# Modulation vectors made inside three other phases, in blocks of 128 columns

## The chip, the cores and the metric

The kernel runs on one core of a Trainium2 chip. The metric is the device time of one execution in microseconds (us): the kernel before took 4822.7 us, the median of three runs (4816.3 to 4823.88). Engines are named as in the profile: PE multiplies matrices (PEld is its weight load), DVE, ACT and POOL work on vectors, and SP starts most transfers (its queue is SPq).

## The reference, cut to what matters

The program is three transformer blocks on 1024 tokens of width 1024. The second block is modulated by a conditioning vector:

```
sc, scc = silu(c), silu(c_ctx)                  # two vectors of 1024
mx = sc @ w_mod + b_mod                         # w_mod is 1024 x 6144
mc = scc @ w_mod + b_mod
sh1, sc1, g1, sh2, sc2, g2 = split(mx, 6)
csh1, csc1 = first two pieces of mc
hc = modulate(rms_norm(ctx, norm1_g), csh1, csc1)      # keys and values of 256 context tokens
hx = modulate(rms_norm(x, norm1_g), sh1, sc1)
x = x + g1 * mixer(hx, ...)                     # attention, long convolution, Fourier mixing
h2 = modulate(rms_norm(x, norm2_g), sh2, sc2)
x = x + g2 * experts(h2)
```

The first block has a gated short convolution, `b * conv3(c * u)` over 256 channels. In the mixer of the second block the heads of queries and keys are each normalised over 64 channels, multiplied by a gain and rotated (`u * cos + rotated(u) * sin`). Its long convolution starts with filters made by a small network with two sine layers, times a decay, and divided by the sum of their absolute values.

## The kernel before, in words

The program is a row of phases. Each phase writes one instruction list for every engine; the lists meet at the phase's end, and the next phase starts after it. Nothing of one phase runs beside the next, so what a phase costs is set by the last of its engines. Semaphores order the work within a phase.

Four stages matter here. The first is `short_conv_phase` (name `conv`, L1603), near the end of the first block: SP loads coefficients and six tiles of 128x1024, DVE does ten operations on them, ACT stores two results. PE has no work in it.

The second is `mod_phase` (`mod`, L1730), ahead of the second block's context. It makes all 6144 columns of both vectors. The weights come in twelve tiles of 128x8x512 (2048 KB each, L1755). For each tile PE holds 128x2 numbers of silu(c) as weights and streams the 128x512 tile past them, eight times (L1779). DVE adds the bias to the 2x512 result (L1798), PE turns it with four small products (L1785), and DVE copies the turned columns into `cols` (L1801), which later phases read as 48 blocks of 128.

The third is three phases in a row: `load_phase` (`b2_tables`, L1590: cosines, sines and two copies of the values), `norm_phase` (`qk_norm`, L290: for each of ten half rows ACT squares, PE sums with a 128x128 matrix of ones blocks at L390, DVE, ACT, ACT and DVE finish), and `rope_phase` (`qk_rope`, L1688: PE moves the pairs at L1706, DVE multiplies and adds, SP stores).

The fourth is `hyena_filter_phase` (`filter`, L1837). PE makes two layers of 64x1024 (L1940); DVE reduces the angles and ACT takes the sine after each (L2047). ACT and POOL split eight raw tables meanwhile (L2032, L2070): ACT's list holds four of those splits ahead of each sine. Then PE goes through eight chunks: filter taps of chunk i (L1955, 64-row weights) and sums of absolute values of chunk i-1 (L1946); DVE multiplies by the decay (L2000) and ACT takes the absolute value (L2063). SP's list starts the tables, the decays and a 4096 KB copy of `xT` to memory (`x_spill`) in a fixed order.

All products in these stages take 32-bit floats. Each such instruction shows as two records on PE and two weight loads in the trace.

Of the kernel before, what the change touches and what calls it, by code (L numbers as in the profile page):

```python
# [11 lines left out]
ALU = mybir.AluOpType  # L12
ACT = mybir.ActivationFunctionType
AX = mybir.AxisListType
P = 128
T = 1024
# [1586 lines left out]
def short_conv_phase(nc, name, n_pairs, src, gate_before, gate_after, w, b, left, out):  # L1603

    n_chunks = 2 * n_pairs
    with Phase(nc, name) as ph:
        taps, bias = ph.sb("taps", [P, n_chunks, 3]), ph.sb("bias", [P, n_chunks])
        z = [ph.sb(f"z{s}", [P, T + 2]) for s in range(2)]  # L1610
        before = [ph.sb(f"before{s}", [P, T]) for s in range(2)]
        after = [ph.sb(f"after{s}", [P, T]) for s in range(2)]
        acc = [ph.sb(f"acc{s}", [P, T]) for s in range(2)]
        coef_loaded, padded = ph.sem("coef_loaded"), ph.sem("padded")
        loaded, used = [ph.sem(f"loaded{s}") for s in range(2)], [ph.sem(f"used{s}") for s in range(2)]
        stored, done = [ph.sem(f"stored{s}") for s in range(2)], ph.sem("done")
        block = ph.block()
        n_in = 1 + (gate_before is not None) + (gate_after is not None)
        n_ops = 3 + (gate_before is not None) + (gate_after is not None)

        @block.sync
        def _(sp):
            for i in range(3):
                sp.dma_start(taps[:, :, i], w[i].rearrange("(c p) -> p c", p=P),
                             allow_slow_non_contiguous=True).then_inc(coef_loaded, 16)
            load_columns(sp, bias[:, :], b, coef_loaded)

            def load(i, s):
                sp.dma_start(z[s][:, left:left + T], src(i * 2 + s)).then_inc(loaded[s], 16)
                if gate_before is not None:  # L1630
                    sp.dma_start(before[s][:, :], gate_before(i * 2 + s)).then_inc(loaded[s], 16)
                if gate_after is not None:
                    sp.dma_start(after[s][:, :], gate_after(i * 2 + s)).then_inc(loaded[s], 16)

            for s in range(2):
                load(0, s)
            if n_pairs > 1:
                with sp.Fori(1, n_pairs) as i:
                    for s in range(2):
                        sp.wait_ge(used[s], i)  # L1640
                        load(i, s)

        @block.vector
        def _(dve):
            for s in range(2):
                if left:
                    nc.vector.memset(z[s][:, 0:left], 0.0).then_inc(padded, 1)
                if left < 2:
                    nc.vector.memset(z[s][:, left + T:], 0.0).then_inc(padded, 1)
            dve.wait_ge(padded, 2 * ((left > 0) + (left < 2)))  # L1650
            dve.wait_ge(coef_loaded, 16 * 4)
            for s in range(2):
                dve.sem_inc(stored[s], 16)
            with dve.Fori(0, n_pairs) as i:
                for s in range(2):
                    op = 0

                    def link(ins):
                        nonlocal op
                        op += 1  # L1660
                        ins.then_inc(done, 1)
                        dve.wait_ge(done, i * (2 * n_ops) + (s * n_ops + op))

                    dve.wait_ge(loaded[s], i * (16 * n_in) + 16 * n_in)
                    if gate_before is not None:
                        link(nc.vector.tensor_tensor(z[s][:, left:left + T], z[s][:, left:left + T], before[s][:, :], ALU.mult))
                    dve.wait_ge(stored[s], i * 16 + 16)
                    tap = lambda n: taps[:, ds(i * 2 + s, 1), n]
                    link(nc.vector.tensor_scalar(acc[s][:, :], z[s][:, 0:T], tap(0), bias[:, ds(i * 2 + s, 1)],
                                                 ALU.mult, ALU.add))  # L1670
                    for n in (1, 2):
                        link(nc.vector.scalar_tensor_tensor(out=acc[s][:, :], in0=z[s][:, n:n + T], scalar=tap(n),
                                                            in1=acc[s][:, :], op0=ALU.mult, op1=ALU.add))
                    if gate_after is not None:
                        link(nc.vector.tensor_tensor(acc[s][:, :], acc[s][:, :], after[s][:, :], ALU.mult))
                    dve.sem_inc(used[s], 1)

        @block.scalar
        def _(act):
            with act.Fori(0, n_pairs) as i:  # L1680
                for s in range(2):
                    act.wait_ge(used[s], i + 1)
                    act.dma_start(out(i * 2 + s), acc[s][:, :].rearrange("p (o t) -> p o t", o=1)).then_inc(stored[s], 16)
            for s in range(2):
                act.wait_ge(stored[s], 16 * n_pairs + 16)
# [44 lines left out]
def mod_phase(nc, name, ident, c_rows, w_mod, b_mod, cols):  # L1730

    N = w_mod.shape[1]
    n_pairs = N // HALF // 2
    w_view = w_mod.rearrange("(c p) n -> p c n", p=P)
    with Phase(nc, name) as ph:
        cond, sig, silu = ph.sb("cond", [P, KD, 2]), ph.sb("sig", [P, KD, 2]), ph.sb("silu", [P, KD, 2])
        w_sb = [ph.sb(f"w{s}", [P, KD, HALF]) for s in range(2)]
        bias = [ph.sb(f"bias{s}", [2, HALF]) for s in range(2)]
        rows = [ph.sb(f"rows{s}", [2, HALF]) for s in range(2)]
        acc = [ph.ps(f"acc{s}", [2, HALF]) for s in range(2)]  # L1740
        turned = [ph.ps(f"turned{s}", [P, 4, 2]) for s in range(2)]
        cond_loaded, sig_ready, silu_ready = ph.sem("cond_loaded"), ph.sem("sig_ready"), ph.sem("silu_ready")
        loaded, acc_ready = [ph.sem(f"loaded{s}") for s in range(2)], [ph.sem(f"acc_ready{s}") for s in range(2)]
        rows_ready, turned_ready = [ph.sem(f"rows_ready{s}") for s in range(2)], [ph.sem(f"turned_ready{s}") for s in range(2)]
        cols_ready = [ph.sem(f"cols_ready{s}") for s in range(2)]
        block = ph.block()

        @block.sync
        def _(sp):
            for r in range(2):  # L1750
                sp.dma_start(cond[:, :, r], c_rows[r].rearrange("(c p) -> p c", p=P),
                             allow_slow_non_contiguous=True).then_inc(cond_loaded, 16)

            def load(i, s):
                sp.dma_start(w_sb[s][:, :, :], w_view[:, :, ds((i * 2 + s) * HALF, HALF)]).then_inc(loaded[s], 16)  # L1755
                for r in range(2):
                    sp.dma_start(bias[s][r:r + 1, :], b_mod[0:1, ds((i * 2 + s) * HALF, HALF)]).then_inc(loaded[s], 16)

            for s in range(2):
                load(0, s)  # L1760
            with sp.Fori(1, n_pairs) as i:
                for s in range(2):
                    sp.wait_ge(rows_ready[s], i)
                    load(i, s)

        @block.scalar
        def _(act):
            act.wait_ge(cond_loaded, 32)
            nc.scalar.activation(sig[:, :, :], cond[:, :, :], ACT.Sigmoid).then_inc(sig_ready, 1)

        @block.tensor
        def _(pe):
            pe.wait_ge(silu_ready, 1)
            with pe.Fori(0, n_pairs) as i:
                for s in range(2):
                    pe.wait_ge(loaded[s], i * 48 + 48)
                    pe.wait_ge(cols_ready[s], i + 1)
                    for c in range(KD):
                        mm = nc.tensor.matmul(acc[s][:, :], silu[:, c, :], w_sb[s][:, c, :], start=(c == 0), stop=(c == KD - 1))  # L1779
                    mm.then_inc(acc_ready[s], 1)  # L1780
                for s in range(2):
                    pe.wait_ge(silu_ready, 1)
                    pe.wait_ge(rows_ready[s], i + 1)
                    for b in range(4):
                        tr = nc.tensor.matmul(turned[s][:, b, :], rows[s][:, b * P:(b + 1) * P], ident[0:2, 0:2],  # L1785
                                              start=True, stop=True)
                    tr.then_inc(turned_ready[s], 1)
# [3020 lines left out]
```

## Time and profile before

| | us |
|---|---|
| median of three runs | 4822.7 |
| the profiled execution | 4812.0 |
| its span, first to last instruction | 4810.1 |
| PE busy | 3956.5 (82%) |
| DVE busy | 2735.6 (57%) |
| ACT busy | 1976.4 (41%) |

The profile is of one execution, whose own time (4812.0) is 1.9 us over its span and 10.7 us under the median. Since phases don't overlap, a stage is read by its own start and end, and by what its engines wait for between them. The granted clock of PE is a number between 0 and 1: 0.50 is 1.2 GHz, 1.00 is 2.4 GHz, and numbers between are stretches with both. The page's own chain of what ended last breaks off after a few per cent, so the stages below are read from the time lines.

### The profile page before, as it was taken

To read this page: it belongs to the slowest core of one execution; us is meant where nothing else is said; L and a number is where in the kernel's file an instruction comes from. 1 tells how busy PE (TensorE), PEld (TensorE's weight loads), DVE (VectorE), ACT (ScalarE), POOL (GpSimd) and SP (SyncE) were. 2 spreads that over 40 slices of the span, in tenths; PEclk is the share of its full clock that TensorE was granted. 3 is DMA by queue.
4 is the path that set the end of the run, shared out by engine and by line. 5 is a ranking of instruction groups with operands and counts; after the bars stand their busy time and mean duration, and the time that the engine had idled before them with its cause. 6 is when DMAs were issued, how large, how long until landed. Compare 5 with 4: busy or idle time off the path is not lost. (4 is left out here: it accounts for less than half of the span.)

```text
span 4810.1 us, 51648 instructions
## 1 busy us (share of the span) xinstructions
PE 3956.5 (82%) x18534; PEld 3124.2 (65%) x18534; DVE 2735.6 (57%) x3196; ACT 1976.4 (41%) x2670; POOL 470.4 (10%) x349
## 2 busy tenths in 40 slices
PE   7995756959997797698948999999996997474489
PEld 5884535427885576386746888888885785353477
DVE  4124756132112676675566999999996322445952
ACT  2113543031112465324315777777774112354323
POOL 1000012015000121200000011000100400000010
PEclk8997878979998899799958999999997998787789
DMA  3223122422222201416318999999995222424241
GB/s 94 96 87 89 49 86 60 158 92 79 96 96 80 58 24 37 163 72 206 101 71 341 401 383 380 382 393 381 382 381 187 78 93 95 157 76 120 54 143 67
DMA packets 437325, 768.37 MB, mean 160 GB/s; under 512 B 104895, under 2 KB 260799, under 8 KB 436024
## 3 DMA queue, kind: packets, MB, share of 16 engines
q1 hardware_dynamic: 406760, 686.74, 40.8%
q10 hardware_dynamic: 25808, 62.92, 3.4%
q0 software_dynamic: 4608, 16.78, 1.3%
q8 instruction: 87, 1.43, 0.1%
q14 instruction: 62, 0.51, 0.0%
HBM read 644.85 MB, written 115.87 MB: 158 GB/s over the span
## 5 line engine op out<-in xcount | busy, mean ns | idle before, releaser
L71 PE MATMUL b_in_acc<-b_in_acts_hi,b_in_w_hi 128*128 128x512 f32 (+1 forms) x1456 | 580.4, 399 | 48.4 <-POOL b_in_acts_lo L749 20.6
L72 PE MATMUL b_in_acc<-b_in_acts_lo,b_in_w_hi 128*128 128x512 f32 (+1 forms) x1456 | 573.7, 394 | 0.0
L73 PE MATMUL b_in_acc<-b_in_acts_hi,b_in_w_lo 128*128 128x512 f32 (+1 forms) x1456 | 573.4, 394 | 0.0
L3354 DVE TENSOR_TENSOR experts_w_lo<-top_xT,experts_w_hi 128x2048 fp32r<-128x2048 f32 x192 | 437.4, 2290 | 62.7 <-ACT experts_w_hi L3299 62.7
L66 DVE CAST b_in_w_hi<-b_in_w 128x1024 fp32r<-128x1024 f32 (+1 forms) x91 | 68.0, 750 | 702.0 <-PE b_in_acc L73 702.0
L3354 DVE TENSOR_TENSOR experts_w_lo<-experts_ring,experts_w_hi 128x2048 fp32r<-128x2048 f32 x192 | 435.8, 2288 | 31.8 <-ACT experts_w_hi L3299 29.6
L559 ACT ACTIVATE b_in_out<-b_in_acc 128x512 f32<-128x512 f32 (+1 forms) x182 | 108.9, 599 | 810.8 <-PE b_in_acc L73 808.7
L3299 ACT ACTIVATE experts_w_hi<-top_xT 128x2048 fp32r<-128x2048 f32 x192 | 367.5, 1919 | 126.9 <-PE experts_gate L73 74.8
L3299 ACT ACTIVATE experts_w_hi<-experts_ring 128x2048 fp32r<-128x2048 f32 x192 | 367.7, 1921 | 115.0 <-PE experts_up L73 65.0
L71 PEld LDWEIGHTS b_in_acc<-b_in_acts_hi,b_in_w_hi 128*128 128x128 f32 (+1 forms) x1456 | 275.6, 189 | 129.3 <-POOL b_in_acts_lo L749 34.8
L73 PEld LDWEIGHTS b_in_acc<-b_in_acts_hi,b_in_w_lo 128*128 128x128 f32 (+1 forms) x1456 | 276.6, 190 | 59.1
L72 PEld LDWEIGHTS b_in_acc<-b_in_acts_lo,b_in_w_hi 128*128 128x128 f32 (+1 forms) x1456 | 276.8, 190 | 56.8 <-issue 0.7
L71 PE MATMUL experts_gate<-experts_w_hi,experts_xg_hi 128*128 128x512 f32 x512 | 202.1, 395 | 4.8 <-DVE experts_w_lo L3354 4.8
L71 PE MATMUL experts_y_ps<-experts_w_hi,experts_act_hi 128*128 128x512 f32 x512 | 205.5, 401 | 0.0
L71 PE MATMUL experts_up<-experts_w_hi,experts_xg_hi 128*128 128x512 f32 x512 | 200.9, 392 | 2.7 <-DVE experts_w_lo L3354 2.7
L73 PE MATMUL experts_gate<-experts_w_hi,experts_xg_lo 128*128 128x512 f32 x512 | 200.5, 392 | 0.0
L73 PE MATMUL experts_y_ps<-experts_w_hi,experts_act_lo 128*128 128x512 f32 x512 | 200.4, 391 | 0.0
L72 PE MATMUL experts_gate<-experts_w_lo,experts_xg_hi 128*128 128x512 f32 x512 | 200.4, 391 | 0.0
L72 PE MATMUL experts_y_ps<-experts_w_lo,experts_act_hi 128*128 128x512 f32 x512 | 199.8, 390 | 0.0
L73 PE MATMUL experts_up<-experts_w_hi,experts_xg_lo 128*128 128x512 f32 x512 | 199.5, 390 | 0.0
L72 PE MATMUL experts_up<-experts_w_lo,experts_xg_hi 128*128 128x512 f32 x512 | 199.5, 390 | 0.0
L1235 ACT ACTIVATE gqa_pT_hi<-gqa_turned 128x512 fp32r<-128x512 f32 (+1 forms) x192 | 94.4, 531 | 86.4 <-PE gqa_turned L1159 86.2
(677 smaller groups left out, 8656.4 us busy)
## 6 DMA issues: line engine op xcount, KB each, us to landing
experts_ring<-in_w_gate SPq DMA_DIRECT2D x128, 1024.0 KB, 7.4
top_xT<-in_w_up SPq DMA_DIRECT2D x128, 1024.0 KB, 9.9
experts_ring<-in_w_down SPq DMA_DIRECT2D x64, 1024.0 KB, 9.6
top_xT<-in_w_down SPq DMA_DIRECT2D x64, 1024.0 KB, 9.3
b_in_w<-in_w_in SPq DMA_DIRECT2D x90, 512.0 KB, 3.9
proj<-b_in_out ACTq DMA_DIRECT2D x90, 512.0 KB, 2.7
mod_w<-in_w_mod SPq DMA_DIRECT2D x12, 2048.0 KB
x_spill<-top_xT SPq DMA_DIRECT2D x3, 4096.0 KB, 14.0
```

The source lines that it names most:

```text
L66: return nc.vector.tensor_copy(hi, x)
L71: nc.tensor.matmul(out, w_hi, x_hi, start=start, stop=False)
L72: nc.tensor.matmul(out, w_hi, x_lo, start=False, stop=False)
L73: return nc.tensor.matmul(out, w_lo, x_hi, start=False, stop=stop)
L559: nc.scalar.activation(out, acc[s][h][0:m, :], ACT.Sigmoid if gated else ACT.Copy).then_inc(ready, 1)
L1235: nc.scalar.activation(pT_hi[m % 2][:, b0:b0 + bn, t0:t0 + P], turned[x % 2][:, 0:bn, :], ACT.Copy).then_inc(hi_ready, 1)
L3299: nc.scalar.activation(w_hi[n % HIS][:, :, :], ring[n % RING], ACT.Copy).then_inc(hi_ready, 1)
L3354: nc.vector.tensor_tensor(w_lo[n % HIS][:, :, :], ring[n % RING], w_hi[n % HIS][:, :, :].bitcast(F32), ALU.subtract).then_inc(lo_ready, 1)
```

## The change

`mod_phase` is gone. `cols`, `silu` and `bias` are now held for the whole run of the first two blocks, and the twelve tiles are made by three other phases, four each. A helper does a block of 128 columns the other way round: the 128x128 block of `w_mod` is PE's weights, and the 128x2 numbers of silu are streamed past. The result lies in columns at once, without a turn.

```
+MOD_STEPS = (4, 4, 4)
+def modulation_block(nc, acc, w, silu, b):
+    for c in range(KD):
+        mm = nc.tensor.matmul(acc, w[:, c, b * P:(b + 1) * P], silu[:, :, c], start=(c == 0), stop=(c == KD - 1))
+    return mm
```

The short convolution's phase becomes `conv_modulation_phase`. It turns the bias and both conditioning vectors with one product, makes silu, and PE does tiles 0 to 3. DVE writes the convolution's result straight into `y`.

```
+        @block.tensor
+        def _(pe):
+            pe.wait_ge(vec_loaded, 48)
+            nc.tensor.transpose(turned[:, :], vec_rows[:, :], ident[0:NB + 2 * KD, 0:NB + 2 * KD]).then_inc(vec_turned, 1)
+            pe.wait_ge(silu_ready, 1)
+            for n in range(n_steps):
+                pe.wait_ge(w_loaded[n % RING], 16 * (n // RING + 1))
+                for b in range(4):
+                    mm = modulation_block(nc, made[n][:, b, :], w[n % RING], silu, b)
+                mm.then_inc(made_ready, 1)
```

SP's list in this phase, before; all of it but the coefficients is the convolution's inputs:

```order
L1624 DMA conv_taps<-in_conv_w 128x2x1 x3
L767 DMA conv_bias<-in_conv_b 128x2x1
L1629 DMA conv_z<-proj 128x1024
L1631 DMA conv_before<-proj 128x1024
L1633 DMA conv_after<-proj 128x1024
```

And now; `conv_w` is a tile of `w_mod`, `conv_vec_rows` holds the bias and the two vectors:

```order
L1643 DMA conv_vec_rows<-in_b_mod 48x128
L1645 DMA conv_vec_rows<-in_c 8x128
L1645 DMA conv_vec_rows<-in_c_ctx 8x128
L1637 DMA conv_w<-in_w_mod 128x8x512
L1641 DMA conv_z<-proj 128x1024
L1641 DMA conv_before<-proj 128x1024
L1641 DMA conv_after<-proj 128x1024
L1649 DMA conv_taps<-in_conv_w 128x2x1 x3
```

The first weight tile now stands ahead of the convolution's inputs, and the fourth waits until PE has done the first.

`query_key_phase` (`qk`) does the work of `b2_tables`, `qk_norm` and `qk_rope` in one phase, half row by half row, with 16 blocks (tiles 4 to 7) spread between its products:

```
+            for j in range(NU):
+                pe.wait_ge(square_ready, j + 1)
+                if j >= 2:
+                    pe.wait_ge(log_ready, j - 1)
+                nc.tensor.matmul(sums[j % 2][:, :], block_ones[:, :], square[j % 2][:, :], start=True, stop=True).then_inc(sums_ready, 1)
+                modulation(part(j, 0))
+                if j >= 1:
+                    rotate(j - 1)
+                modulation(part(j, 1))
+            rotate(NU - 1)
```

PE's list here, before and now, the first rows; `qk_sums` is the sum of squares, `qk_moved` the rotation, `qk_made` a modulation block:

```order
-L381 UNCONDITIONAL_BRANCH
-L390 MATMUL qk_norm_sums<-qk_norm_square,top_squares 128x512 x10
-L39 UNCONDITIONAL_BRANCH
-L1701 UNCONDITIONAL_BRANCH
-L1706 MATMUL qk_rope_moved<-b2q_qk,top_squares 128x512 x10
+L1790 UNCONDITIONAL_BRANCH
+L1812 MATMUL qk_sums<-qk_square,top_squares 128x512
+L1609 MATMUL qk_made<-modulation_silu,qk_w 128x2 x8
+L1812 MATMUL qk_sums<-qk_square,top_squares 128x512
+L1609 MATMUL qk_made<-modulation_silu,qk_w 128x2 x8
+L1806 MATMUL qk_moved<-qk_xn,top_squares 128x512
+L1609 MATMUL qk_made<-modulation_silu,qk_w 128x2 x8
```

The two runs of ten products become a mixture with eight small products after nearly every large one. ACT now takes the logarithm of the sums directly (scale 1/64, added eps), and DVE's ten mean operations are gone.

`hyena_filter_phase` gets tiles 8 to 11 as eight half tiles of 1024 KB. The loads stand in SP's list, and PE calls `modulation(n)` after each of the two layers and in chunks 1 to 6:

```
             for c in range(2):
                 load_line(c)
+            for n in range(2):
+                load_mod(n)
             for j in range(4):
                 load_raw(j)
+            load_mod(2)
             for i in range(2):
                 load_decay(i)
...
                 if i >= 1:
                     sizes(i - 1)
+                if i in (1, 2, 3, 4, 5, 6):
+                    modulation(i + 1)
...
+            dve.wait_ge(mod_used, 2 * n_steps)
+            nc.vector.tensor_tensor(cols[...], made[:, :, :], mod_bias[...], ALU.add).then_inc(cols_made, 1)
```

PE's list in the filter phase, before, from the first layer; `filter_pre` is a layer, `filter_norm` the sum of absolute values:

```order
L1940 MATMUL filter_pre<-filter_feats,filter_w 64x512 x2
L1940 MATMUL filter_pre<-filter_hidden,filter_w 64x512 x2
L1955 MATMUL filter_taps<-filter_w,filter_hidden 128x512 x4
L1946 MATMUL filter_norm<-filter_size,top_squares 128x512 x2
L1955 MATMUL filter_taps<-filter_w,filter_hidden 128x512 x2
```

And the same stretch now:

```order
L2060 MATMUL filter_pre<-filter_feats,filter_w 64x512 x2
L1609 MATMUL filter_made<-modulation_silu,filter_mod_w 128x2 x16
L2060 MATMUL filter_pre<-filter_hidden,filter_w 64x512 x2
L1609 MATMUL filter_made<-modulation_silu,filter_mod_w 128x2 x16
L2076 MATMUL filter_taps<-filter_w,filter_hidden 128x512 x4
L2067 MATMUL filter_norm<-filter_size,top_squares 128x512 x2
L1609 MATMUL filter_made<-modulation_silu,filter_mod_w 128x2 x16
L2076 MATMUL filter_taps<-filter_w,filter_hidden 128x512 x2
```

Sixteen small products now stand between the sums of one chunk and the taps of the next, six times.

## Rows read from the trace of the kernel before

**Rows 1.** The page, its head and part 1: busy us, share, instructions.

```profile
span 4810.1 us, 51648 instructions
PE 3956.5 (82%) x18534; PEld 3124.2 (65%) x18534; DVE 2735.6 (57%) x3196; ACT 1976.4 (41%) x2670; POOL 470.4 (10%) x349
```

**Rows 2.** Windows: the four stages, from their first instruction to the next stage's.

```profile
core 0: us, PE busy (x) PEld busy (x) DVE busy (x) ACT busy (x) POOL busy (x), PEclk, DMA share, GB/s
663.29:687.35 24.06, 0.00 (x0) 0.00 (x0) 11.76 (x12) 0.00 (x0) 0.00 (x0) 0.50 0.48 175
886.59:994.28 107.69, 96.30 (x288) 26.80 (x288) 10.32 (x25) 1.50 (x2) 0.00 (x0) 0.95 0.68 234
1516.64:1583.00 66.36, 30.10 (x40) 8.67 (x40) 32.74 (x50) 18.97 (x31) 0.00 (x0) 0.66 0.28 105
1908.84:1996.76 87.92, 45.03 (x74) 14.64 (x74) 72.20 (x63) 27.30 (x25) 23.89 (x8) 0.67 0.56 199
```

**Rows 3.** Time line of mod: start us, us, engine, line, operation, records [idle before].

```profile
887.64 0.57 SPq L1755 DMA_DIRECT2D mod_w<-in_w_mod  x1
896.23 15.23 PE L1779 MATMUL mod_acc<-mod_w,mod_silu 128*2 128x512 f32 x32 [10.64 <-DMA mod_bias<-in_b_mod]
991.73 1.95 PE L1785 MATMUL mod_turned<-top_squares,mod_rows 2*128 2x2 f32 x16
```

**Rows 4.** Time line and windows of the two long runs of small products.

```profile
2426.04 27.49 PE L3069 MATMUL route_logits<-route_w,b2r_hT 128*128 128x16 f32 x128 [16.20 <-DMA route_w<-in_w_router]
2514.23 27.44 PE L3091 MATMUL route_picked<-route_facts,route_sel 128*128 128x4 f32 x128 [4.64 <-DVE route_sel L3149]
2426.04:2453.53 27.49, 27.49 (x128) 27.38 (x128) 0.00 (x0) 0.00 (x0) 0.00 (x0) 0.50 0.27 116
2514.23:2541.67 27.44, 27.44 (x128) 27.36 (x128) 15.27 (x7) 0.00 (x0) 0.00 (x0) 0.50 0.00 1
```

**Rows 5.** Time line of PE in the last phase: eight small records, twice.

```profile
4688.22 0.95 PE L4297 MATMUL last_col<-top_squares,last_square 128*128 128x1 f32 x8
4694.81 1.87 PE L4297 MATMUL last_col<-top_squares,last_square 128*128 128x1 f32 x8 [2.75 <-ACT last_square L4382]
```

**Rows 6.** Time line of conv: DVE's first product, the next phase's first load.

```profile
663.29 1.41 SPq L1624 DMA_DIRECT2D conv_taps<-in_conv_w  x3
671.79 1.23 DVE L1666 TENSOR_TENSOR conv_z<-conv_z,conv_before 128x1024 f32<-128x1024 f32 x1 [8.32 <-DMA conv_after<-proj]
687.35 1.14 SPq L1088 DMA_DIRECT2D mem_k_raw<-mem_kv  x2
```

**Rows 7.** Time line and window of the norm and rotation.

```profile
1548.81 1.10 PE L390 MATMUL qk_norm_sums<-qk_norm_square,top_squares 128*128 128x512 f32 x2 [1.10 <-ACT qk_norm_square L352]
1579.32 0.69 DVE L1719 TENSOR_TENSOR qk_rope_out<-qk_rope_cos_part,qk_rope_sin_part 128x512 f32<-128x512 f32 x1
1563.00:1577.00 14.00, 9.26 (x16) 2.37 (x15) 13.76 (x23) 0.00 (x0) 0.00 (x0) 0.94 0.27 112
```

**Rows 8.** Time line of the filter phase.

```profile
1922.08 1.06 ACT L2032 ACTIVATE hy_table_hi<-filter_raw 128x1024 fp32r<-128x1024 f32 x1 [1.47 <-DMA filter_raw<-in_half_tables]
1926.20 1.06 ACT L2032 ACTIVATE hy_table_hi<-filter_raw 128x1024 fp32r<-128x1024 f32 x1 [0.26 <-DMA filter_raw<-in_half_tables]
1929.79 1.06 ACT L2047 ACTIVATE filter_hidden<-filter_hidden 64x1024 f32<-64x1024 f32 x1 [1.23 <-DVE filter_hidden L1833]
1948.64 1.06 ACT L2047 ACTIVATE filter_hidden<-filter_hidden 64x1024 f32<-64x1024 f32 x1 [2.28 <-DVE filter_hidden L1833]
1949.75 7.19 PE L1955 MATMUL filter_taps<-filter_w,filter_hidden 64*128 64x512 f32 x8 [15.18 <-ACT filter_hidden L2047]
1960.91 1.99 PE L1955 MATMUL filter_taps<-filter_w,filter_hidden 64*128 64x512 f32 x4
1987.30 3.31 PE L1946 MATMUL filter_norm<-filter_size,top_squares 128*128 128x512 f32 x4 [2.78 <-ACT filter_size L2063]
1990.72 0.69 DVE L2015 TENSOR_SCALAR filter_total<-filter_norm 128x512 f32<-128x512 f32 x1 [3.24 <-PE filter_norm L1946]
```

More of the change, by code:

```diff
@@ L1608, in short_conv_phase @@
     with Phase(nc, name) as ph:
-        taps, bias = ph.sb("taps", [P, n_chunks, 3]), ph.sb("bias", [P, n_chunks])
+        taps, taps_bias = ph.sb("taps", [P, 2, 3]), ph.sb("taps_bias", [P, 2])
         z = [ph.sb(f"z{s}", [P, T + 2]) for s in range(2)]
[L1611 to L1614, printed above, removed]
@@ L1615, in short_conv_phase @@
-        loaded, used = [ph.sem(f"loaded{s}") for s in range(2)], [ph.sem(f"used{s}") for s in range(2)]
-        stored, done = [ph.sem(f"stored{s}") for s in range(2)], ph.sem("done")
+        before, after, acc = ([ph.sb(f"{n}{s}", [P, T]) for s in range(2)] for n in ("before", "after", "acc"))
+        vec_rows, sig = ph.sb("vec_rows", [NB + 2 * KD, P]), ph.sb("sig", [P, 2 * KD])
+        w = [ph.sb(f"w{s}", [P, KD, HALF]) for s in range(RING)]
+        turned = ph.ps("turned", [P, NB + 2 * KD])
@@ L1635, in _ @@
[L1635 to L1641, printed above, removed]
+            load_columns(sp, taps_bias[:, :], taps_b, coef_loaded)
+            load_w(1)
+            load_chunk(1)
+            for n in range(2, n_steps):
+                load_w(n)
+        @block.tensor
[8 more added lines that the diff above has]
+                mm.then_inc(made_ready, 1)
@@ L1651, in _ @@
-            dve.wait_ge(coef_loaded, 16 * 4)
-            for s in range(2):
[L1653 to L1676, printed above, removed]
@@ L1678, in _, with squares @@
         @block.scalar
         def _(act):
[L1680 to L1685, printed above, removed]
+            act.preload_act_table_set("natural_log_exp_and_others")
+            def squares(j):
+                act.wait_ge(x_loaded[j // 2], 16)
+                if j >= 2:
+                    act.wait_ge(sums_ready, j - 1)
+                nc.scalar.activation(square[j % 2][:, :], x[j // 2][:, at(j)], ACT.Square).then_inc(square_ready, 1)
@@ L1727, in _ @@
             sp.wait_ge(stored, 16 * len(chunks))
[L1730 to L1787, printed above, removed]
-        @block.vector
-        def _(dve):
-            dve.wait_ge(sig_ready, 1)
-            nc.vector.tensor_tensor(silu[:, :, :], sig[:, :, :], cond[:, :, :], ALU.mult).then_inc(silu_ready, 1)
-            for s in range(2):
-                dve.sem_inc(cols_ready[s], 1)
-            with dve.Fori(0, n_pairs) as i:
-                for s in range(2):
-                    dve.wait_ge(acc_ready[s], i + 1)
-                    nc.vector.tensor_tensor(rows[s][:, :], acc[s][:, :], bias[s][:, :], ALU.add).then_inc(rows_ready[s], 1)
-                for s in range(2):
-                    dve.wait_ge(turned_ready[s], i + 1)
-                    nc.vector.tensor_copy(cols[:, ds((i * 2 + s) * 4, 4), :], turned[s][:, :, :]).then_inc(cols_ready[s], 1)
@@ L1908, in _ @@
                 load_line(c)
+            for n in range(2):
+                load_mod(n)
             for j in range(4):
                 load_raw(j)
+            load_mod(2)
             for i in range(2):
@@ L1934, in _, with modulation @@
         def _(pe):
+            def modulation(n):
+                pe.wait_ge(mod_loaded[n % 3], 16 * (n // 3 + 1))
+                for b in range(2):
+                    mm = modulation_block(nc, made[:, 2 * n + b, :], mod_w[n % 3], silu, b)
+                mm.then_inc(mod_used, 1)
             pe.wait_ge(loaded, 16 * 7)
```

247 lines of the change are left out of this document (208 added, 39 removed).

## The prediction

> **What bounds the kernel now.** I read the page's head first: PE is busy 82% of the span [rows 1]. That is a mean over stages; what counts here are four stages which the change touches, so I took windows over them [rows 2]. The reader is to see that PE does nothing in conv (24.1 us), is busy in nearly all of mod (96.3 of 107.7 us), and is busy in about half of the other two (30.1 of 66.4 and 45.0 of 87.9). The phases don't overlap, so 107.7 us can go, if the work fits into PE's free time elsewhere: 24.1 + 36.3 + 42.9, together 103 us. The question is how long this work takes in its new form, and for that I looked for the nearest products in the time line: 128x128 weights with a few columns streamed [rows 4, 5]. Last I read the time lines of the receiving stages for what their ends wait for [rows 6 to 8].
>
> **What a block costs.** In mod one record with 512 columns comes each 0.43 us (16 of a tile in 7; the first 32 took 15.23 with a slow start) [rows 3]. The new form has 8 products for a block of 128 columns, 16 records, 64 for a tile, 768 for all. The nearest run is `route_logits`: 128x128 float weights, 16 columns streamed, sums over eight pieces; 128 records in 27.49 us, 0.215 us each. `route_picked`, with 4 columns, takes 27.44 [rows 4]. Both ran at a granted clock of 0.50 (1.2 GHz) from first to last, with no idle time in them. At 1.00 (2.4 GHz) the same kind costs half: eight `last_col` records take 0.95 us, 0.12 each, against 1.87 after 2.75 us of idleness [rows 5], and 16 turns with 2 columns in mod take 1.95, after 0.25 for the last to come out about 0.114 each [rows 3]. So a tile costs 64 x 0.215 = 13.8 us at the low level and 64 x 0.114 = 7.3 at the high one; all twelve cost 165 or 88 us. The low price alone is over the 107.7 that goes.
>
> Which level? PE idles before conv, before the queries' phase and before the filters, all three begin at the low level [rows 2, 6, 8], and both route runs stayed there for 27 us though PE never paused [rows 4]. I take the low level for runs of small products.
>
> The Trainium skill ("TensorE: Matmul & The Clock Gate", "Why this matters for your kernels") advises to keep TensorE continuously busy to get the full clock. Read so, conv's 256 records would lift it; route's rows speak against this, since weight loads and matmuls there were back to back at 0.50. The same page's section "LDWEIGHTS (loading the stationary operand)" gives a load's time by its columns alone, about 107 ns for 128; by two such loads for a float product even the high clock would leave 0.21 us a record. Rows 5 differ with 0.12, and the measurement decides.
>
> **Part by part.** *mod removed*: -107.7 us, from its first load to the next phase's [rows 2]. What follows it waits for its own load and starts at the low level either way.
>
> *conv*: now three small loads stand first, so the first tile's load is issued at 663.3 + 3 x 0.47 = 664.7. In mod the tile's load was issued at 887.64 and PE began at 896.23, 8.6 us later [rows 3]; so PE begins here at 673.3. The turn and silu are done by then (their three loads are small). The second tile has 13.8 us to come, behind 1.5 MB of inputs; 2 MB take about 5.5 us at the rate of the filter's raw tables (three steps of 0.5 MB from 1922.08 to 1926.20, 1.37 each [rows 8]), so PE doesn't wait again. Four tiles: 55.0, to 728.3; DVE's last addition and the change of phase 0.7, to 729.0. The stage takes 65.7, **+41.6 us**. The convolution's DVE work (11.8 us [rows 2]) lies beside it, and costs nothing. At the high level it would be 29.2 for the tiles, +16.
>
> *queries and keys*: loads of x, gains (0.6 each) and the first tile are issued by 1519.5; with mod's 8.6 the first block starts at about 1527.5 to 1528. Behind it PE has 16 blocks x 3.44 = 55.0 and 19 large products (sums 1 to 9 and ten rotations) of two records. A record with 512 columns takes 0.857 at the low level (7.19 us for eight, less 0.33 for the last to come out [rows 8]) and 0.43 at the high (1.99 for four); so 19 x 1.71 = 32.5. PE is the bound: DVE needs 4 operations of about 0.7 for a half row, ACT three of 0.6, against 8.8 on PE. PE ends at 1615.0, two DVE operations later (1.7) the last store is issued, and it needs the same 3.0 us to the next phase as before (1579.32 + 0.69 to 1583.00 [rows 2, 7]). Next phase at 1619.7, +36.7. The rounds which I merge (two phase changes, ten mean operations, gains that came last) are in this, since I build the stage anew. A large product now seldom has another beside it, only three times are two together. In the norm the level was high for short stretches after such runs (1.10 us for two records [rows 7]), so I take off 4: **+33 us**. With all at the high level: 16 x 1.83 + 19 x 0.86 = 45.6 behind 1527.5, the end at 1577.8, -5.
>
> Rotation's window shows that PE can keep the high level with pauses, once it has it (9.3 of 14 us busy, 0.94 [rows 7]); a small product streams 2 columns where those streamed 512, so I don't count on it.
>
> *filters*: first the loads. Two half tiles (2 MB, 5.5 us) go ahead of the raw tables and a third ahead of the decays and the 4 MB copy. ACT's fourth table split moves from 1926.20 to 1931.7, with the table load and its own time the first sine starts at 1934.1 instead of 1929.79; the second, behind the last four tables, 8 us later: 1956 instead of 1948.64. It costs 7.5 because ACT's list keeps the splits ahead of the sine; DVE's angles, which were the last to come, are early now. modulation(0) and (1) lie in PE's waits for the sines and cost nothing. Then the loop: first taps at 1957.3; 8 x 4 + 8 x 4 records of 0.857 are 54.9, six half tiles of 6.9 are 41.3; PE ends at 2053.5, and after the same 6.1 us (1990.6 to 1996.76) the phase at 2059.6: +62.9 with all at the low level. Before, the loop was at the high level from 1960.9 on (1.99 us for four), and low again at 1987.30 after 2.78 us of idleness [rows 8]. Now 6.9 us of large records stand together in each round. I estimate that in two rounds of three the level rises at their end and is lost within the 6.9 us of small ones, with about 3.4 saved each time: 14 off, **+49 us**. High throughout: 7.1 us a round, +25.
>
> Sum: -107.7 + 41.6 + 33 + 49 = **+16 us**. The profiled execution would go from 4812.0 to 4828, and the median, 10.7 above it, to 4839.
>
> **Rivals.** *The small products run high beside large ones.* In conv PE stays low, in the other two stages the large products lift the clock and it holds: -107.7 + 41.6 - 5 + 25 = -46, 4777. For it: rotation's window and the loop's high level. Against it: the level was gone after 2.78 us without a product [rows 8]. The sign of the whole turns where a tile's mean cost falls by 16/12 = 1.3 us, to 12.5.
>
> *Every run of small products is lifted*, conv's too, as the rule cited would have it: -107.7 + 16 - 5 + 25 = -72, 4751. Against it stand both route runs. It decides more than anything else here: 88 us for the small products or 165.
>
> *The loads bind.* The clock never rises in the three stages, and the filter's half tiles, with pieces of 1 KB instead of 2, come more slowly: +42 + 37 + 63 = 142, or +34 with the removal, and up to 10 more if the second sine moves by as much; 4857 to 4867.
>
> *No change*: the filter's loop is high in each round's large part (-22 instead of -14), queries 10 off: about +2 to +5, 4826.
>
> **How the numbers follow.** Low level with some rises 0.60 (its own range 4825 to 4858), loads and no rises 0.12, near no change 0.10, high beside large products 0.12, high everywhere 0.06. The likeliest gives 4839. The range goes from 4788 to 4866: it leaves out the last and most of the one before, and a little above. About 0.2% (9.6 us) is what a measurement can tell: faster 0.20, same 0.15, slower 0.65.
>
> **What would show it.** conv 65 us long, PE busy in 55 of it at a clock of 0.50, 256 small records with 0.215 from one to the next. The queries' phase 98 to 103 us, clock under 0.65, PE busy through. First and second sine 4 and 7 us later against the phase's start; rounds of 11 to 13.7 us in the loop; the filter phase 125 to 150. Wrong it is if the clock in conv is near 1.00, or if the merged phases end under 80 us.

## The result and the profile after

The changed kernel took 4826.0 us (median of 20 runs, 4815.7 to 4833.2) against 4819.1 for the kernel before (20 runs, 4809.7 to 4831.1). The ratio is 1.0016 with a 95% interval of 1.0009 to 1.0023: slower by some 7 us. That is less than the 0.2% (9.6 us) which the prediction had set as what can be told, though the interval lies wholly above 1. The forecast was +16. The profiled execution took 4825.94 us. Its page, head and part 1, to be held against [rows 1]:

```profile
span 4824.2 us, 52429 instructions
PE 4035.5 (84%) x19015; PEld 3257.8 (68%) x19015; DVE 2707.3 (56%) x3173; ACT 1974.8 (41%) x2669; POOL 463.5 (10%) x349
```

Windows over the three stages that are left, with the columns of [rows 2]: conv, queries and keys, filters.

```profile
665.79:730.48 64.69, 55.11 (x257) 54.87 (x257) 12.71 (x18) 0.18 (x1) 0.00 (x0) 0.50 0.50 180
1452.60:1549.40 96.80, 83.13 (x296) 62.49 (x296) 28.49 (x45) 19.86 (x31) 0.00 (x0) 0.54 0.43 159
1875.90:2014.50 138.60, 108.89 (x330) 67.58 (x330) 56.74 (x64) 27.11 (x25) 18.69 (x8) 0.56 0.52 187
```

The columns to read are the length, PE's busy time and the granted clock behind POOL's column. The four stages took 286.0 us before [rows 2]; these three take 300.1. The difference, 14.1, is the whole difference of the two spans (4824.2 - 4810.1). In all three the clock is at or near 0.50, the lower level (1.2 GHz).

PE's time line in conv. The first tile is there 9.2 us after the stage began, and 256 records follow without a pause, 0.214 us each, as route's did [rows 4]:

```profile
667.94 0.36 PE L1660 MATMUL conv_turned<-top_squares,conv_vec_rows 64*128 64x64 f32 x1 [6.97 <-DMA conv_vec_rows<-in_c_ctx]
675.04 54.75 PE L1609 MATMUL conv_made<-modulation_silu,conv_w 128*128 128x2 f32 x256 [6.74 <-DMA conv_w<-in_w_mod]
```

PE's time line in the queries' and keys' phase, around one of the two places where the level rose. A block (16 records) takes 3.41 us, a large product 2.06; after two large ones together the next two blocks take 2.17 and 2.39, and then the level is low again:

```profile
1463.77 3.57 PE L1609 MATMUL qk_made<-modulation_silu,qk_w 128*128 128x2 f32 x16 [5.07 <-DMA qk_w<-in_w_mod]
...
1479.29 3.41 PE L1609 MATMUL qk_made<-modulation_silu,qk_w 128*128 128x2 f32 x16
1482.56 2.06 PE L1806 MATMUL qk_moved<-qk_xn,top_squares 128*128 128x512 f32 x2
1484.41 1.91 PE L1812 MATMUL qk_sums<-qk_square,top_squares 128*128 128x512 f32 x2
1486.12 2.17 PE L1609 MATMUL qk_made<-modulation_silu,qk_w 128*128 128x2 f32 x16
1488.14 1.10 PE L1806 MATMUL qk_moved<-qk_xn,top_squares 128*128 128x512 f32 x2
1489.08 2.39 PE L1609 MATMUL qk_made<-modulation_silu,qk_w 128*128 128x2 f32 x16
1491.34 2.05 PE L1812 MATMUL qk_sums<-qk_square,top_squares 128*128 128x512 f32 x2
```

PE's time line in the filters, a round of the loop at the low level and one in which the small products run at the high one. The rounds are 14.04 and 11.0 us long, and the four records of the taps take 3.78 where before they took 1.99 [rows 8]:

```profile
1945.87 6.83 PE L1609 MATMUL filter_made<-modulation_silu,filter_mod_w 128*128 128x2 f32 x32
1952.62 3.78 PE L2076 MATMUL filter_taps<-filter_w,filter_hidden 64*128 64x512 f32 x4
1956.33 3.78 PE L2067 MATMUL filter_norm<-filter_size,top_squares 128*128 128x512 f32 x4
1959.91 6.83 PE L1609 MATMUL filter_made<-modulation_silu,filter_mod_w 128*128 128x2 f32 x32
...
1973.95 4.08 PE L1609 MATMUL filter_made<-modulation_silu,filter_mod_w 128*128 128x2 f32 x32
1977.96 3.50 PE L2076 MATMUL filter_taps<-filter_w,filter_hidden 64*128 64x512 f32 x4
1981.39 3.78 PE L2067 MATMUL filter_norm<-filter_size,top_squares 128*128 128x512 f32 x4
1984.96 3.71 PE L1609 MATMUL filter_made<-modulation_silu,filter_mod_w 128*128 128x2 f32 x32
```

### The profile page after: what moved, and what is told of

Same layout as the page of the kernel before. It is cut to its first block and busy times, and to the rows that moved or that the text cites. A ratio compares the mean times of both kernels' runs of the same rounds, so it can differ in the third digit from the quotient of the medians.

```text
span 4824.2 us, 52429 instructions
## 1 busy us (share of the span) xinstructions
PE 4035.5 (84%) x19015; PEld 3257.8 (68%) x19015; DVE 2707.3 (56%) x3173; ACT 1974.8 (41%) x2669; POOL 463.5 (10%) x349
## 6 DMA issues: line engine op xcount, KB each, us to landing
x_spill<-top_xT SPq DMA_DIRECT2D x3, 4096.0 KB, 13.7
```

## The stages of every kernel that was profiled

Each number is a stage's length in us in one profiled execution, from its first instruction to the next stage's first. The names of the kernels are explained with the experiments.

| kernel | conv | mod | queries, keys | filters | sum |
|---|---|---|---|---|---|
| before | 24.1 | 107.7 | 66.4 | 87.9 | 286.0 |
| before, second | 24.4 | 115.5 | 66.5 | 87.8 | 294.2 |
| before, third | 24.1 | 111.9 | 65.3 | 96.0 | 297.3 |
| after | 64.7 | - | 96.8 | 138.6 | 300.1 |
| after, second | 64.6 | - | 96.5 | 135.8 | 296.9 |
| after, third | 64.7 | - | 96.7 | 141.0 | 302.4 |
| merge alone | 24.1 | 107.6 | 42.9 | 87.6 | 262.2 |
| 128 columns in conv | 46.4 | - | 93.4 | 141.1 | 280.9 |
| 128 columns in all | 46.3 | - | 63.8 | 110.4 | 220.5 |
| 64 columns in all | 64.8 | - | 63.7 | 110.1 | 238.6 |
| 16 columns in all | 64.6 | - | 96.8 | 140.8 | 302.2 |
| 128, loads later | 44.8 | - | 63.6 | 108.2 | 216.6 |

## Experiments

**Both kernels again.** No edit. Each kernel was profiled and timed once more, and then profiled in a third execution. They tell how far one profile speaks for a kernel. What was expected of the kernel before:

> The kernel before once more, as it is. It tells how far the profiled execution of before (4812.0 us, its stages 24.1 conv, 107.7 mod, 66.4 norm and rotation, 87.9 filters) speaks for other executions. Theory A (the four stages repeat, what differs is spread over stages that the change leaves alone): time ratio 1.000, the four stages within 2 us of these numbers in sum, whatever the whole execution takes. Theory B (one of the four stages of before is usually longer, because the level of the clock comes at other moments, and the first profile had a lucky one): the four together 5 to 10 us longer than 286.0, which would explain why the timed change is about 7 us where the two profiles differ by 14.

and of its third execution:

> The kernel before once more, one look. mod_phase took 107.7 us in one of its executions, 115.5 in another (the level fell for short stretches in five of six pairs of tiles), and 107.6 in merge_only, where the same phase stands. If both are usual, this look has one of them or a number between; conv 24, norm and rotation 66.4, filters 88 again within 0.5. If 115.5 was a rare disturbance, 107.7.

Measured: the second had a ratio of 1.0004 (0.9995 to 1.0013), 4816.0 us; the profiled executions' spans were 4815.8 and 4821.0. The four stages were not 286.0 but 294.2 and 297.3. Windows over mod in the second and, in another fence, over mod and the filters in the third:

```profile
882.20:997.70 115.50, 104.41 (x288) 27.91 (x288) 10.32 (x25) 1.50 (x2) 0.00 (x0) 0.88 0.63 218
```

```profile
887.50:999.40 111.90, 101.18 (x288) 27.36 (x288) 10.32 (x25) 1.50 (x2) 0.00 (x0) 0.91 0.64 225
1913.20:2009.20 96.00, 53.37 (x74) 16.95 (x74) 72.44 (x63) 27.34 (x25) 23.29 (x8) 0.59 0.51 182
```

The same records, a clock of 0.88 and 0.91 where it was 0.95 [rows 2], and PE busy for 104.4 and 101.2 us instead of 96.3. The time line of the second shows it by pairs of tiles: 32 records that took 14.0 at the high level take 15.59 in four pairs.

```profile
910.89 15.59 PE L1779 MATMUL mod_acc<-mod_w,mod_silu 128*2 128x512 f32 x32 [0.35 <-DMA mod_bias<-in_b_mod]
926.41 1.95 PE L1785 MATMUL mod_turned<-top_squares,mod_rows 2*128 2x2 f32 x16
928.42 13.97 PE L1779 MATMUL mod_acc<-mod_w,mod_silu 128*2 128x512 f32 x32
```

In the third, the filters' loop reached the high level only at the taps of chunk 4, not of chunk 2 as in [rows 8]:

```profile
1976.84 3.78 PE L1946 MATMUL filter_norm<-filter_size,top_squares 128*128 128x512 f32 x4
1980.55 2.41 PE L1955 MATMUL filter_taps<-filter_w,filter_hidden 64*128 64x512 f32 x4
1982.89 1.98 PE L1946 MATMUL filter_norm<-filter_size,top_squares 128*128 128x512 f32 x4
```

So Theory B held in kind, with 8 and 11 us where it had 5 to 10: the first profile was of an execution in which the touched stages were short. The expectation for the third, which had the filters at 88 again, missed: they too vary. The rest of the program is not fixed either: outside the four stages these three executions took 4524.1, 4521.6 and 4523.7 us.

Of the changed kernel the second execution was expected to show:

> The changed kernel once more, as it is. Theory A: ratio to before 1.001 to 1.002, stages again 64.7 (conv), 96.8 (queries and keys) and 138.6 (filters), within 1 us each but for the level's flips: in the filters three rounds of six were 3.3 us shorter, and if these flips come by chance the filters' stage would move by 3.3 or 6.6 us between executions. Theory B (the changed stages repeat exactly): 300.1 in sum to within 1 us, and the three short rounds are the same three.

and the third:

> The changed kernel once more, one look: conv 64.7 within 0.2; queries and keys 93 to 97; filters 135.8, 138.6 or 141 by the number of rounds in the loop of which the small products run at the high level (four, three or two of six, 3.3 us each); sum of the three 293 to 302, against 286 or 294 for the four stages of before. So a change between 0 and +16 us from one pair of executions to another, around a mean of about 8, as timed.

Measured: ratio 1.0025 (1.0015 to 1.0035); stages 296.9 and 302.4. Conv repeats to 0.1 us, queries and keys to 0.3; the filters move by about 2.8 us with each round whose small products run high (four of six in the second). In the third they took 141.0 with three such rounds; there the last eight records of the sums took 6.48 us instead of 4.87. The queries' and keys' phase moves too: with the same instructions it took 93.4 in the kernel "128 columns in conv" below. The means of three executions are 292.5 before and 299.8 after, +7.3; pair by pair the stages give +14.1, +2.7 and +5.1. The timed changes are +6.9, in the second set +11.3 (4823.8 against 4812.6 for 25 executions of before, or +7.9 against the 4816.0 of the 11 others), and in the third, of single executions, +11.4 and +15.4 (4834.3 against 4822.9 and 4818.9). The second pair ran on one chip and the third on another, so what share of the spread is the chip's is not told apart.

**The merge alone.** The kernel before, with one of the change's parts: the three phases of the queries and keys in one, without modulation.

```
-            load_phase(nc, "b2_tables", ...)
-            norm_phase(nc, "qk_norm", ...)
-            rope_phase(nc, "qk_rope", ...)
+        query_key_phase(nc, "qk", block_ones, C["pair_rot"], rows_of(p, Q2, 5), ..., rows_of(q) + [kx[:, 0:T]], copies)
```

> The kernel before with one part of the change alone: tables, norm and rotation of the queries and keys are one phase as in the changed kernel, but with no modulation in it; mod_phase, conv and the filters stay as before. The prediction put a gain of the merge only into its total for that stage (33 longer with four tiles at 13.8 in it). Theory A (the merge saves two phase changes and DVE's ten mean operations, and the coefficients come beside the tables; then DVE bounds it with four operations of 0.7 to 0.8 for each of ten half rows): stage 50 to 55 us instead of 66.4, ratio to before 0.997. Rival (with PE's products interleaved with waits the level stays low, sums and rotations alternate on a chain through four engines): 60 to 66, ratio 0.999 to 1.000. It also gives a third look at mod_phase, which was 107.7 in one execution of before and 115.5 in the other: Theory B expects one of these two or a value between.

Measured: 4790.1 us, ratio 0.9956 (0.9942 to 0.9969); the stage took 42.9, less than Theory A gave. Its window, and DVE's groups by line (busy us, mean ns | idle before):

```profile
1515.80:1558.70 42.90, 23.45 (x40) 7.46 (x40) 27.41 (x41) 19.76 (x31) 0.00 (x0) 0.82 0.42 162
```

```profile
L1792 DVE SCALAR_TENSOR_TENSOR qk_xn<-qk_x,qk_gains,qk_inv 128x512 f32<-128x512 f32 x10 | 7.5, 751 | 10.9 <-DMA qk_sin<-in_grid_sin 7.8 <-ACT qk_inv L1753 1.9
L1781 DVE TENSOR_TENSOR qk_out<-qk_cos_part,qk_sin_part 128x512 f32<-128x512 f32 x10 | 6.9, 693 | 1.0
```

DVE waits 7.8 us for the sine table and then goes with hardly a gap, some 3.0 us for a half row. PE's time line in the middle of the stage: the large products are at the high level, with 1.0 us of waiting in each round.

```profile
1537.06 1.12 PE L1761 MATMUL qk_moved<-qk_xn,top_squares 128*128 128x512 f32 x2 [1.02 <-DVE qk_xn L1792]
1538.03 1.02 PE L1767 MATMUL qk_sums<-qk_square,top_squares 128*128 128x512 f32 x2
```

The estimate of 50 to 55 had left DVE's start where it was. What follows is a price for the modulation in this phase: 96.8 - 42.9 = 53.9 us for four tiles, 13.5 each, the low level's price for the small products (13.7). That is a net price, since it holds the large products' slowing too, and what the small ones fill of PE's waits. The stage's +30.4 in the result is +53.9 for the modulation and -23.5 for the merge. All three places together pay 40.6 + 53.9 + 50.7 = 145 us for what mod did in 108 to 116.

**More columns in conv.** The changed kernel, but each small product streams its two columns 64 times over. Same weights, same number of records; the surplus lands in PSUM beside the wanted columns, and later blocks write over it.

```
-def modulation_block(nc, acc, w, silu, b):
+REPEATS = (64, 1, 1)
+def modulation_block(nc, made, at, w, silu, b, repeats):
     for c in range(KD):
-        mm = nc.tensor.matmul(acc, w[:, c, b * P:(b + 1) * P], silu[:, :, c], start=(c == 0), stop=(c == KD - 1))
+        moving = silu[:, :, c:c + 1].rearrange("p r o -> p o r").to_broadcast([P, repeats, 2])
+        mm = nc.tensor.matmul(made[:, 2 * at:2 * at + 2 * repeats].rearrange("p (k r) -> p k r", r=2),
+                              w[:, c, b * P:(b + 1) * P], moving, start=(c == 0), stop=(c == KD - 1))
```

> As the changed kernel, but in conv each small product streams its two columns 64 times over (128 columns instead of 2, the same weights, the same 256 records; the surplus lands in PSUM beside the wanted columns and is overwritten or left). Theory A (what keeps PE at 1.2 GHz in runs of small products is that so little is streamed; the loads of weights alone don't lift the level): PE reaches the high level in conv, its 256 records take 30 to 36 us instead of 54.75, the phase 40 to 46 instead of 64.7, the whole 20 us less than the changed kernel (4803 to 4808, ratio to before 0.997). Theory B (float products with 128x128 weights stay low as in the router, or PE has been idle too long before this phase): conv 64.7 again, ratio 1.0016 as for the changed kernel. Theory C (streaming more costs by the column): a record of 128 columns at the low level needs 0.214 us by the quarter of the 0.857 us for 512, so as much as now, and no more than 2 us are lost.

Measured: 4803.6 us, ratio 0.9982 (0.9973 to 0.9991). Conv took 46.4 instead of 64.7. PE's time line there:

```profile
669.01 9.63 PE L1611 MATMUL conv_made<-modulation_silu,conv_w 128*128 128x128 f32 x64 [6.50 <-DMA conv_w<-in_w_mod]
680.13 7.41 PE L1611 MATMUL conv_made<-modulation_silu,conv_w 128*128 128x128 f32 x64 [1.49 <-DMA conv_w<-in_w_mod]
689.39 16.19 PE L1611 MATMUL conv_made<-modulation_silu,conv_w 128*128 128x128 f32 x128 [1.85 <-DMA conv_w<-in_w_mod]
```

The second tile takes 7.41 us instead of 13.7: the small record is at 0.116 and the level is high. Sixty-four times the streamed data, and the time is halved. PE now waits 1.5 and 1.9 us for weights, the new second limit. Theories B and C are out.

**More columns everywhere.** The one line that differs is `REPEATS = (64, 64, 64)`.

> As wide_conv, with 128 columns streamed in all three phases. Theory A: conv -20, the queries' and keys' phase from 96.8 to about 66 (16 blocks at 1.83 instead of 3.41 and the large products at 0.86 instead of 1.71), the filters from 138.6 to 110 to 115; the whole 65 to 75 us under the changed kernel, 4750 to 4760, ratio to before 0.986 to 0.988, faster than before. Theory B: the same as the changed kernel within 3 us. A mixture (high only in conv, where nothing interrupts the run; in the other two the waits between the products break it): 4795 to 4805.

Measured: 4740.7 us (4737.6 to 4743.3), ratio 0.9849 (0.9835 to 0.9862), so 1.5% faster than before and 83 us under the changed kernel, more than the 65 to 75 of Theory A (its own parts add up to 75 to 80). The windows:

```profile
660.40:706.70 46.30, 33.56 (x257) 32.83 (x257) 12.62 (x18) 0.18 (x1) 0.00 (x0) 0.82 0.69 251
1428.50:1492.30 63.80, 50.22 (x296) 38.66 (x296) 27.89 (x45) 19.86 (x31) 0.00 (x0) 0.85 0.63 241
1817.90:1928.30 110.40, 78.18 (x330) 49.46 (x330) 56.71 (x64) 27.21 (x25) 18.68 (x8) 0.78 0.66 235
```

In the queries' phase blocks of 1.95 us stand between large products of 1.02 to the end; in the filters' loop it is 3.74 for a half tile between sums and taps of 1.99, rounds of 7.41 us. PE's time line, two rows of the one and then a round of the other:

```profile
1456.66 1.95 PE L1611 MATMUL qk_made<-modulation_silu,qk_w 128*128 128x128 f32 x16
1458.45 1.02 PE L1815 MATMUL qk_sums<-qk_square,top_squares 128*128 128x512 f32 x2
...
1889.68 3.74 PE L1611 MATMUL filter_made<-modulation_silu,filter_mod_w 128*128 128x128 f32 x32
1893.35 1.99 PE L2079 MATMUL filter_taps<-filter_w,filter_hidden 64*128 64x512 f32 x4
1895.27 1.98 PE L2070 MATMUL filter_norm<-filter_size,top_squares 128*128 128x512 f32 x4
```

The same instruction counts as in the result's windows, at clocks of 0.78 to 0.85 instead of 0.50 to 0.56.

**Sixteen and sixty-four columns.** `REPEATS = (8, 8, 8)` and `(32, 32, 32)`.

> As wide_all, but 16 columns streamed. Theory A (the level goes by what is streamed): nearly as the changed kernel with its 2, since the router's run with 16 columns stayed at 0.50: conv 64 to 65, ratio to before 1.001 to 1.002. The rival to it (it is not the amount, but that the moving operand is repeated or that the result is contiguous over many columns which made wide_all fast): as wide_all, 0.985.

> As wide_all, but 64 columns streamed instead of 128. If the high level needs streamed columns in proportion, the level is reached in part and the whole lies between 4741 and 4824; if 64 are enough it is 4741 within 5 us, with a small record at 0.114 as before, since its weight load then is what sets its time. The loss would be seen first in conv, where no large product helps.

Measured with 16: 4824.0 us, ratio 1.0017 (1.0008 to 1.0027), as the changed kernel; so the repeated operand and the longer rows in PSUM are not the cause; the kernels with 16 and with 128 columns differ in the number of columns streamed, and the room for them in PSUM, alone. With 64: 4759.7 us, ratio 0.9893 (0.9879 to 0.9908), neither the 4741 that 64 columns would give if they were enough everywhere nor the changed kernel's time. Of the stages the difference to 128 is conv alone, which stayed low from end to end while the two stages with large products between were as with 128. Windows over conv, first with 16 and then with 64 columns:

```profile
659.40:724.00 64.60, 55.13 (x257) 54.87 (x257) 12.71 (x18) 0.18 (x1) 0.00 (x0) 0.50 0.49 180
```

```profile
660.00:724.80 64.80, 55.21 (x257) 54.86 (x257) 12.70 (x18) 0.18 (x1) 0.00 (x0) 0.50 0.49 179
```

PEld is busy 54.9 of these 64.6 us, with weight loads back to back, and the level did not rise.

**The filters' loads elsewhere.** As with 128 columns in all, and in SP's list:

```
-            for n in range(2):
-                load_mod(n)
             for j in range(4):
                 load_raw(j)
-            load_mod(2)
+            for n in range(2):
+                load_mod(n)
...
             for j in range(4, NJ):
                 load_raw(j)
+            load_mod(2)
```

> As wide_all, with the modulation's loads in the filters' phase put elsewhere in SP's list: the first two half tiles behind the first four raw tables instead of ahead of them, the third behind the last four raw tables instead of ahead of the 4 MB copy. It tests the step on the sines (4 and 7 us later than in before by prediction, 4.0 and 4.3 measured). Theory A (the first sine is late by the 2 MB ahead of the raw tables, the second only by all the bytes ahead of the last tables): first sine 4 us earlier against the phase's start than in wide_all (21 instead of 25.2), the second 2.5 earlier (1 MB less ahead of it; 42 instead of 44.4), the phase 2 to 3 shorter, 108 instead of 110.4. Rival (the second sine waits for the first and for DVE's angles): both 4 earlier, the phase 106. Time 4738, no difference to wide_all that can be told from the whole.

Measured: 4737.3 us, ratio 0.9845 (0.9831 to 0.9859), not to be told from the version before it in the whole. Against the phase's start (1818.3) the sines stand at 20.8 and 42.2, as Theory A had it, and the phase takes 108.2. ACT's time line:

```profile
1836.62 1.28 ACT L2178 ACT_TABLE_LOAD   x1
1839.08 1.06 ACT L2178 ACTIVATE filter_hidden<-filter_hidden 64x1024 f32<-64x1024 f32 x1 [1.17 <-DVE filter_hidden L1935]
...
1859.58 1.06 ACT L2163 ACTIVATE hy_table_hi<-filter_raw 128x1024 fp32r<-128x1024 f32 x1 [0.24 <-DMA filter_raw<-in_half_tables]
1860.54 1.04 ACT L2178 ACTIVATE filter_hidden<-filter_hidden 64x1024 f32<-64x1024 f32 x1
```

The first sine waits for DVE's angles again, as in [rows 8]; the second follows the last raw table's split.

## Why the prediction went wrong, step by step

**What bounds it, and the level.** The step on the price held: low level for the small products, 0.214 us a record (0.215 predicted), 13.7 a tile. In conv the weights loaded back to back did not lift the level. The Trainium skill ("TensorE: Matmul & The Clock Gate", "Why this matters for your kernels") asks for a continuously busy TensorE; conv's rows, busy 54.75 us without a gap at 0.50, go against reading that as instructions back to back; with 128 columns streamed by the same records the level rose. The prediction's other sentence on that page gave 0.21 us a record from two weight loads for each. The windows show one load beside each record (x257 and x257 in conv), and not whether it stands for two passes. Either way a load time that leaves the clock out does not fit, since the record took 0.214 us at the low level and 0.116 at the high one. No term of the sum used it.

**Conv.** +41.6 predicted, +40.6 measured; the first tile came 9.25 us behind the stage's start, not 10.0. **Queries and keys.** +33 predicted, +30.4 measured; the flips of the level saved about 6 us, not 4. The prediction did not part the two things in this term: the merge gains 23.5 by itself, and the modulation costs 53.9.

**Filters.** +49 predicted, +50.7 measured, out of two errors. The first sine came 4.0 us later against the phase's start, as forecast (4.3), and the second 4.3 us, not 7.5. So the first taps stood 45.2 us behind the phase's start (1921.13 - 1875.90) instead of the 48.5 forecast. The two sines and the first taps in the changed kernel, to be held against [rows 8]:

```profile
1900.85 1.06 ACT L2175 ACTIVATE filter_hidden<-filter_hidden 64x1024 f32<-64x1024 f32 x1
1920.04 1.04 ACT L2175 ACTIVATE filter_hidden<-filter_hidden 64x1024 f32<-64x1024 f32 x1
1921.13 7.19 PE L2076 MATMUL filter_taps<-filter_w,filter_hidden 64*128 64x512 f32 x8 [8.58 <-ACT filter_hidden L2175]
```

The second batch of tables waits for the bytes ahead of it, and two 4 us delays don't add up; the last experiment moved the two sines by 4.4 and 2.2. From the first taps on the phase took 93.4 us, where 88 had been forecast: I had four rounds of six saving 3.4 us each; it was three saving 3.1, and 2.3 at the last sums (eight records in 4.87), while a round at the low level took 14.04 us and not the 13.8 of the sum. The picture itself held: the level rose behind the large products, it was the small ones that ran at the high level (4.08 and 3.71 us for 6.83), and the large ones stayed at 3.5 to 3.8.

**The step that failed** is in the sum, "-107.7 + 41.6 + 33 + 49 = **+16 us**": the term for what is removed, "*mod removed*: -107.7 us", was mis-sized, and so was the base of 87.9 on which the filters' +49 was built. I took both from one execution as fixed, and carried "the median, 10.7 above it" over unchanged. Mod took 107.7, 115.5 and 111.9 us (mean 111.7) and the filters 87.9, 87.8 and 96.0 (mean 90.6), by when the level rises and falls. The change removes or drowns just these stages, so the part of the distance that lay in them goes with them.

In numbers: the four stages before have a mean of 292.5 and not 286.0, which is 6.5 of the 8.7 us between +16 and the +7.3 of the means; the other 2.2 are the new stages, 299.8 where 302.0 was forecast. The timed runs agree: the profiled execution of before (4812.0) lay 7.1 us under the median of 20 runs, that of the changed kernel (4825.9) on its median. So this pair of profiles has +14.1, close to the forecast, and the medians +6.9. Of the 13 us between 4839 and 4826.0, 3.6 come from the base as well: 4822.7 was the median of three runs, 4819.1 that of 20.

The sign was right and the measured time lies in the range; the size was twice too large, since it was made from one execution with short stages. That three means come within 0.4 us of the first timed change is in part luck: the rest of the program took 4520.1 to 4530.1 us in the three profiles of the changed kernel, and the second set of timed runs has +11.3.

**The rivals.** "Every run of small products is lifted" was priced at 40, 61 and 113 us for the three stages (24.1 + 16, 66.4 - 5, 87.9 + 25). It did not come with this change, but with 128 columns it did: 46.4, 63.8, 110.4. I had named the level as what decides more than anything, and held it for given; it could be chosen. "The loads bind" did not happen: in all three stages only the first small product waited for its weights. "No change" had 4826, the very number measured, but by a way that did not come: it had the loop's large products at the high level and 10 us off the queries, and they ran at 3.78 us for four records, with 6 off. Its number is luck. The argument against the first rival, that the level was gone after 2.78 us without a product [rows 8], is a little too strong: the four sums behind that pause took 3.31 us and not 3.78, so the level fell shortly behind it.

Why the high level comes with 128 columns in conv and not with 64 is open beyond these rows; no other widths were tried. Nor was mod's own form, the vectors as weights and the tile streamed (7.0 us a tile at the high level), tried in the three new places.

**The signs.** Conv was as described. The queries' phase took 96.8 us where 98 to 103 was named, and the loop's rounds 10.7 to 14.0 where 11 to 13.7 was; the clock in both (0.54, 0.56) and the filters' 138.6 were as named.

## What to carry to other kernels

Small products next to large weights are priced at the low level of the clock unless a run shows otherwise, and that price can be changed: stream more columns past the same weights, even useless ones, as long as the load of the weights and not the stream sets the record's time. Here 128 columns were worth 83 us of 4824, 64 gave 64 us and 16 gave nothing; so the number has to be tried. A change that bundles a good part (the merge, -23.5 us in its stage) with a bad one (145 us for 108 to 116) shows only the difference; run the parts alone. And before one profile's stage is taken as the cost of what will be removed, look at a second one, above all where the granted clock in it lies between the two levels.

## What the runs showed of the hardware

- A record of 128x128 float weights takes 0.214 us at the low level whether 2, 16 or 64 columns are streamed (PE busy 55.11, 55.13 and 55.21 us in conv), and 0.116 at the high level with 128 columns. At the high level a block of 16 records took 1.84 us with 2 columns (1508.54 in the third execution of the changed kernel), 1.89 with 64 and 1.95 with 128. So streaming cost next to nothing up to these widths.
- The same phase with the same instructions takes 107.7, 111.9 or 115.5 us in different executions, by the level alone. The Trainium skill ("TensorE: Matmul & The Clock Gate", "What's actually happening") says that the ramp is run-variable and calls its penalty less than 1% of a typical kernel. It says the first of the ramp at a kernel's start; here the level moved in the middle of a run. The traces agree on both: 11 us between the three sums of before are 0.2% of the span. For a change of 7 us that is more than the whole effect.
- In the merged phase without modulation the level was high and held through waits of 1.0 us between products; with 2-column products in the place of these waits it was low for most of the phase. Filling PE's gaps with 2-column work made the large products beside it slower, 2.06 us instead of 1.02; with 128 columns in the same places they took 1.02 again.
